# The order of three attention passes on TensorE, and x turned in whole blocks: a two-block transformer on one Trainium2 core

## The reference, cut to what matters

```python
def swa_mixer(x, w_qkv, q_gain, k_gain, sinks, w_o):      # layer 2 of the first block: the local attention
    q, k, v = split(x @ w_qkv)                            # 16 heads of 64, 4 key heads, 256 tokens
    s = q @ band(k).T * 64**-0.5 - slope * dist           # window of 128 tokens
    probs = softmax([s, sink])[..., :-1]
    return (probs @ band(v)) @ w_o

def second_block(x, mem, ...):                            # the last phase
    h = rms_norm(x, g_pre)
    # three branches of attention on projections of h:
    #   a: three dilated windows (128,1), (512,4), (2048,16), 8 heads of 64 each, merged by softmax of their lse
    #   b: 8 heads of 64 over 2 key heads, axial rope
    #   m: 4 heads of 128 over a memory of 256 tokens
    merged = sigmoid(mg0)*ya + sigmoid(mg1)*yb + sigmoid(mg2)*ym
    return x + rms_norm(merged @ w_out, g_post)
```

## Time and profile before

| | |
|---|---|
| median of 3 runs | 2505.98 us (2505.77 to 2507.32) |
| span of the profiled execution, first to last instruction | 2505.3 us |
| PE busy | 2485.4 us, 99% |
| PEld busy | 2278.0 us, 91% |
| DVE busy | 1823.0 us, 73% |
| ACT busy | 1294.7 us, 52% |
| granted TensorE clock, mean | 0.998 |

### The profile page before, as it was taken

One profiled execution on the slowest core, in us unless ns is written; L12 is line 12 of the kernel. 1 busy time (PEld: TensorE's weight loads), 2 busy tenths in 40 slices (PEclk: granted clock), 3 DMA queues, 4 the chain that ended last, 5 costly groups with the idle time before them and its releaser, 6 DMA issues.

```text
span 2505.3 us, 41816 instructions
## 1 busy us (share of the span) xinstructions
PE 2485.4 (99%) x17552; PEld 2278.0 (91%) x17552; DVE 1823.0 (73%) x2203; ACT 1294.7 (52%) x1476; POOL 29.3 (1%) x62
## 2 busy tenths in 40 slices
PE   9999999999999999999999999999999999999999
PEld 8889998898898988988888889888999889999999
DVE  7857678677856777678567876785867868788755
ACT  5545365455534565465466554654535555444643
POOL 0000000000000000000000000000000000011000
PEclk9999999999999999999999999999999999999999
DMA  7554345554544355545543554455424554445352
GB/s 268 200 202 178 110 151 191 202 184 169 201 176 161 141 180 193 194 169 189 201 148 123 186 203 183 171 199 202 170 101 175 199 202 168 169 144 173 139 194 85
DMA packets 62270, 438.04 MB, mean 175 GB/s; under 512 B 7536, under 2 KB 7664, under 8 KB 10128
## 3 DMA queue, kind: packets, MB, share of 16 engines
q1 hardware_dynamic: 59472, 426.95, 47.1%
q0 software_dynamic: 2624, 8.52, 1.1%
HBM read 431.25 MB, written 1.05 MB: 173 GB/s over the span
## 4 chain that ended last, share of the span: by engine, by line
PE 92%; DVE 4%; ACT 2%; issue 1%; DMA 0%; SPq 0%; DVEq 0%; ACTq 0%
PE ps L756 19%; PE ps L838 13%; PE ps L851 12%; PE ps L869 11%; PE ps L840 7%; PE ps L857 6%; PE ps L774 6%; PE ps L870 5%; PE ps L790 2%; PE ps L872 1%; PE ps L873 1%; PE ps L874 1%; ACT w_hi L1395 1%; DVE w_lo L1857 1%; PE ps L938 1%
## 5 line engine op out<-in xcount | busy, mean ns | idle before, releaser
L1857 DVE TENSOR_TENSOR w_lo<-raw,w_hi 128x2048 fp32r<-128x2048 f32 x404 | 924.5, 2291 | 284.5 <-ACT w_hi L1395 275.5
L1395 ACT CAST w_hi<-raw 128x2048 fp32r<-128x2048 f32 x404 | 770.5, 1908 | 530.1 <-PE ps L870 214.3
L756 PE MATMUL ps<-right,w_hi 128*128 128x256 f32 x2112 | 391.3, 285 | 0.1
L756 PEld LDWEIGHTS ps<-right,w_hi 128*128 128x128 f32 x2112 | 332.2, 192 | 3.2 <-issue 1.7
L756 PE MATMUL ps<-right,w_lo 128*128 128x256 f32 x1056 | 298.7, 283 | 0.0
L869 PE MATMUL ps<-hidden,w_hi 128*128 128x512 f32 x768 | 269.3, 393 | 0.0
L838 PE MATMUL ps<-left,w_hi 128*128 128x512 f32 x736 | 256.7, 395 | 1.8 <-DVE left L1913 1.8
L838 PE MATMUL ps<-right,w_hi 128*128 128x512 f32 x736 | 256.7, 395 | 0.2 <-DVE right L2035 0.2
L1938 DVE TENSOR_TENSOR scratch<-ps,scratch 128x512 f32<-128x512 f32 x176 | 121.7, 691 | 155.7 <-ACT scratch L1431 155.7
L870 PE MATMUL ps<-hidden,w_lo 128*128 128x256 f32 x768 | 214.3, 279 | 0.0
L1448 ACT CAST hidden<-scratch 128x256 fp32r<-128x256 f32 x128 | 52.0, 406 | 300.8 <-DVE scratch L1946 300.8
(11 more groups left out here) (356 smaller groups left out, 4499.2 us busy)
## 6 DMA issues: line engine op xcount, KB each, us to landing
raw<-weights_dram SPq DMA_DIRECT2D x404, 1024.0 KB, 4.8
scratch<-scratch POOLq DMA_DIRECT2D x48, 64.0 KB, 1.9
raw<-weights_dram SPq DMA_DIRECT2D x2, 512.0 KB, 5.6
x<-x_t_dram SPq DMA_DIRECT2D x2, 512.0 KB, 7.3
scratch<-c_second_dram POOLq DMA_DIRECT2D x1, 1024.0 KB, 10.5
scratch<-p_t_dram POOLq DMA_DIRECT2D x4, 256.0 KB, 3.1
scratch<-mem_t_dram POOLq DMA_DIRECT2D x1, 1024.0 KB, 6.7
out_dram<-scratch SPq DMA_DIRECT2D x4, 256.0 KB, 2.6
```

The costliest lines, as they stand in the source:

```text
L756: last = nc.tensor.matmul(bank(e, ring)[:, half * T:(half + 1) * T], l, r, start=(place == 0 and j == 0 and half == 0), stop=(place == KC ...
L1395: nc.scalar.copy(w_hi[:, m % SPLIT, :], raw[:, m % RAW, :]).then_inc(weights_hi, 1)
L1857: V.tensor_tensor(w_lo[:, m % SPLIT, :], raw[:, m % RAW, :], w_hi[:, m % SPLIT, :].bitcast(F32), ALU.subtract).then_inc(weights_split, 1)
```

## The change

In the local attention `values(g-1)` is put ahead of `turn(g)`. In the last phase `turn(u)` is put ahead of `values(u-1)`, in all three stretches. `RES` goes from 4 to 2, so that tokens lie as all even ones, then all odd ones; masks, rope tables and the order of the output follow. `turn_x` issues per chunk two whole transposes of 128x128 in place of four products of a 64-token block with the identity.

```diff
-RES = 4
+RES = 2
@@ sw
                 for g in range(7):
                     scores(g + 2)
-                    turn(g)
                     if g:
                         values(g - 1)
+                    turn(g)
                 values(6)
@@ second, stretches one and two, then three
+                        turn(u)
                         values(u - 1)
-                        turn(u)
                         scores(u + 1)
...
                     project(n0 + 27 + u, e0 + 27 + u, XG, ring=2)
+                    turn(u)
                     values(u - 1)
-                    turn(u)
                     scores(u + 1)
@@ turn_x
-                        for r in range(RES):
-                            cols = slice(r // 2 * T + c % 2 * P, r // 2 * T + (c % 2 + 1) * P)
-                            last = nc.tensor.matmul(ps[head_half(r), 4 + u, cols], token_order(x[:, c])[:, r], ident,
-                                                    start=True, stop=True)
+                        for b in range(TB):
+                            cols = slice(b * T + c % 2 * P, b * T + (c % 2 + 1) * P)
+                            last = nc.tensor.transpose(ps[:, 4 + u, cols], token_order(x[:, c])[:, b], ident)
```

## The result

| | median | runs | lowest to highest |
|---|---|---|---|
| before | 2506.06 us | 8 | 2505.40 to 2507.32 |
| changed | 2512.59 us | 8 | 2511.47 to 2513.96 |

The ratio is 1.0025, with a 95% interval of 1.0016 to 1.0033. The changed kernel is 6.5 us slower; repeated in e1 it was 5.3 us slower. Forecast were +4.35 us and a range that ended at 2512.3, which the time missed by 0.3 us. The profiled execution of the changed kernel took 2511.47 us and has a span of 2509.6 us. So 1.9 us lie around the span, and it is 1.8 to 2.1 us in all executions of both kernels of which span and time are known.

What follows compares the result with a forecast made beforehand. PE, busy 99% of 2505.3 us, was taken to bound the kernel. +0.5 - 0.3 + 1.45 + 0.4 + 3.0 - 0.7 = +4.35 us gave 2510.3 us (chance 0.55), range 2507.5 to 2512.3.

Steps and rivals of the forecast that it cites:

- Stretch one, +1.45: Last phase, first stretch: step 1 loses 1.75 us, steps 3 and 4 save 0.3; +1.45 us, bounds 1.2 to 1.8.
- Stretch three, +3.0: Last phase, third stretch: turnings wait for probabilities, DVE's take delays low and logits; +3.0 us, bounds 2.0 and 3.5.
- Stretch two, +0.4: Last phase, second stretch: three turnings wait about 0.2 us each, two save 0.14; +0.4 us, bounds -0.2 and +0.8.
- Local attention, +0.5: Local attention: 1.0 us gained up to scores(7), 0.59 and 0.99 lost at the loop's end; +0.5 us, bounds -0.6 and +1.3.
- x, -0.7: First output projection: shorter turning of x, gain limited by waiting for DVE's third operand pair; -0.7 us, bounds -0.8 and 0.
- Sum of squares, -0.3: Line 809: stride 2 speeds the two matmul records on PE's path; -0.3 us, between nothing and 0.55 us gained.
- Shape changes, 0.14 each: PE in last phase and local attention: each tile-shape change removed saves 0.14 us, bounds 0.09 and 0.17.
- The base: Whole kernel: the runs' median stands 0.68 us above the profiled span of 2505.3 us.
- the second: Rival, stretch three: DVE's lateness goes on in steps 4 and 5, about 1 us each; +6.4 us, 2512.4, chance 0.17.
- The third: Rival, local attention and last phase: shape changes count and waits vanish; with x and sums -2.8 us, 2503.2, chance 0.08.
- the fourth: Rival: DVE catches up after step 1 of stretch three (+1.1), local attention gains (-0.1); +1.85 us, 2507.8, chance 0.2.

Runs made afterwards that it cites:

- e1: The changed kernel again with no edit: 2512.21 us, ratio 1.0020 to the kernel before.
- e2: The changed kernel with five products that nobody reads ahead of the waiting turning in step 1 of stretch one: 2511.15 us.
- e3: The changed kernel with values(0) ahead of turn(1) again in step 1 of stretch one alone: 2509.38 us.
- e4: The changed kernel with values ahead of turning again in stretch three: 2508.43 us.
- e9: The changed kernel with take(u-1) behind low and logits(u+1) on DVE in stretch three: 2510.06 us, ratio 1.0019 to the kernel before.
- e6: The kernel before with only values(g-1) ahead of turn(g) in the local attention: 2506.85 us, 0.1 below before.
- e7: The changed kernel with values first only for local-attention groups 1 to 4, turning first only in steps 3 and 4 of stretch one: 2502.67 us, ratio 0.9985 to before.
- e10: e9 with PE's order in stretch three turn(u), scores(u+1), values(u-1): 2511.42 us, ratio 1.0020 to the kernel before.
- e5: The kernel before with RES = 2 and the whole transposes in turn_x, orders as before: 2505.43 us, ratio 0.9997.
- e8: e7 with four products that nobody reads ahead of the wait about 800 us, in the matrix-memory mixer: 2501.60 us, ratio 0.9980 to before.

## Why the prediction was wrong

The time was missed by 0.3 us at the upper end of the range. The traces have +5.46 against the forecast +4.35: stretch one 1.65 us dearer, local attention and sum of squares together 0.7 cheaper, the rest within 0.1. The other 1.1 us up to the measured +6.5 are told of at the end of this section. By its steps:

- **Stretch one, +1.45: failed.** The wait and the price of the moved values were right (the turning's wait grew by 1.78 us, the forecast lost 1.75). The step that failed is "the values follow it ... 1.79 us": it took their duration from a stretch at clock 1.00 and put it behind a wait of 2.7 us. It was 3.19 us, the scores took 0.28 us more too, and step 1 cost +3.4 us (the next projection from 2200.89 to 2202.55, in an execution 1.70 ahead). Stretch one came to +3.1, and its bounds of 1.2 to 1.8 did not hold it. e1 shows that this recurs, e2 that it stays away when the wait is filled, e3 that the step's old order takes it away. No rival had it: that a wait has a price on the work behind it was in none of them.
- **Stretch three, +3.0: right**, in its place, its mechanism (the `take` ahead of `low` and the logits) and its size of 3.05. e4 takes the whole away. e9 takes the `take` out of the way and 1.15 us with it; in step 3 `low`, waiting for ACT, then stands in its place.
- **Stretch two, +0.4: right**, at +0.5, by three waits of about 0.2 us as named.
- **Local attention, +0.5: mis-sized**, it was 0.0. The loop's end lost 1.42 us where I had 1.58 (0.59 and 0.99), and the steps ahead gained 1.43 where I had 1.0: nothing of that gain was given back ahead of the end. In before PE had waited 0.62, 0.26 and 0.26 us there, and after the change it doesn't. e6 has no change either.
- **x, -0.7: right** at -0.73, ended by the wait for DVE that was named. The transposes themselves cost more than I took (0.66 against 0.42 us), and this did not matter, since the wait absorbs it.
- **Sum of squares, -0.3: mis-sized**, it was -0.49. The rule of the Trainium skill (SBUF — State Buffer, note on cachelines) asked for the whole of it, and line 809 fell to 389 ns against the 379 of an unstrided sum: the rule was the better guide, and the trace had already agreed with it. The whole is 0.48 us by the earlier trace rows, twice 621 less 379 ns, and not the 0.55 that I wrote.
- **Shape changes, 0.14 each: right** (0.14 and 0.16 in steps 3 and 4).
- **The base.** I took 0.68 us around the span, from the median and the profile; it is 1.8 to 2.1. The profiled execution of before was thus one of about 2507.3 us, the longest of the first three. This did no harm to the forecast, which comes to the median of the runs plus the sum. The median of the 33 runs of before beside e1 is 2506.89, and that and +5.46 give 2512.35, against 2512.21 measured.

Of the rivals, the second (lateness goes on in steps 4 and 5) is false: turning 3's step ends at +4.93 us, and the first output projection starts at +4.95. Its time, 2512.4, was nearly met by luck, by another mechanism. The third fell with the waits of line 1146, the fourth with those of stretch three.

The 1.1 us between the first comparison's +6.5 and the +5.46 of the traces most likely come from which executions the two medians fall on. The times of a kernel lie in two groups. Of the 33 runs of before beside e1, 16 lie from 2505.21 to 2506.36 us and 17 from 2506.89 to 2508.18, none between. Of the first comparison's 8 runs of before five lie in the lower group (up to 2506.13), so the median is theirs; of the 8 of the changed kernel two lie at 2511.47 and 2511.66 and six from 2512.44 up, so that median is of the upper one. Middle against middle, the lower groups differ by 5.65 us and the upper by 5.66. With +5.65 the time would have been 2511.7, inside the range: stretch one is the step that failed, but it took this as well to pass the range's end, by 0.3 us. One profile per kernel can't show it, so it is argued.

What stays open: why the clock fell behind the 1.75 us in e3 and not in the other five profiles with that wait.

## What to carry to other kernels

Work that stands ahead of a wait is free as far as it covers the wait; before moving it, read when its successor's input is ready, and move it only in the steps where that input is early (e7 does, and is 2.9 us faster than before by the traces, where the whole change is 5.5 slower). Then follow the moved piece to its reader: here a copy that waited for it headed DVE's queue, and 1.15 of the 3.0 us of stretch three hung on it. And price a TensorE wait that grows to 2 or 3 us at more than its length, because the work behind it may run at the lower clock: here 1.6 us more behind one of 2.69.

## What the runs showed of the hardware that I had not expected

The wait of 2.69 us in stretch one was followed by a fall of the granted clock in all five profiles that have it (after, e1, e4, e9, e10), never in those where it is shorter (0.91 in before, e3 and e5 to e8, 0.53 behind useless work in e2). The one of 1.75 us in stretch three was followed by a fall once (e3) and by none in five profiles. A fall cost about 1.6 us.

Unchanged code isn't equal from one execution to the next. About 800 us every profile has a low clock, but it falls differently. In before (first two lines) and after (last two), a window and the wait behind it:

```profile
796.00:802.00 6.00, 4.00 (x22) 3.17 (x20) 5.13 (x11) 3.69 (x6) 0.00 (x0) 1.00 0.53 190
802.08 2.57 PE L1098 MATMUL ps<-scratch,common 4*128 4x256 f32 x8 [2.08 <-DVE scratch L2324]
```
```profile
796.00:802.00 6.00, 5.78 (x24) 4.54 (x22) 4.86 (x10) 3.81 (x5) 0.00 (x0) 0.74 0.54 198
802.54 1.96 PE L1098 MATMUL ps<-scratch,common 4*128 4x256 f32 x8 [0.76 <-DVE scratch L2323]
```

In before, e1, e2, e4 and e10 the clock is 1.00 up to the wait, the wait is 2.1 us, and the clock falls behind it. In after, e3, e5, e6, e7 and e9 it is 0.72 to 0.74 in the six us ahead: the slower work ahead takes the place of most of the wait, which is 0.45 to 0.76 us, and where the local attention begins these executions are ahead of all of the first kind, by 0.9 to 2.0 us. So a fall ahead of a wait can be hidden by it, and one behind it isn't. In after the stretch turns 0.5 us behind into 1.2 us ahead, the -1.20 us of the table. In ten of these eleven the first kind has a time in the upper group of its kernel and the second one in the lower (e7's times show no two groups), so this looks like part of the 2 to 3 us by which executions of one kernel differ.

Four transposes whose stationary operand is read with stride 2 take 0.66 us, where eight contiguous ones take 0.85 and four contiguous ones of the local attention 0.41 (1310.43 to 1310.84 in before); as a moving operand the stride of 2 is nearly free (389 against 379 ns).
